# A two-part transformer block in fp32: a stage's first tile pair block by block, output projections opened with three column tiles by parts, the last products of the conv layer in token halves

## What is computed

```python
def first_block(x, ...):                        # two layers, h = h + rmsnorm(y)
    y = dilated_mixer(rmsnorm(h), w_in, w_out)  # proj = u @ w_in (10240 columns); rope; windowed attention
                                                # y = o * silu(gate);  y @ w_out
    y = diff_mixer(rmsnorm(h), w_in, ..., w_out)  # differential attention, 8 heads; norm of the heads; y @ w_out
def second_block(x, ...):                       # two layers, x = layer_norm(ALPHA * x + y) twice
    y = hybrid_mixer(x, ...)                    # sparse attention (top 128 keys) and a gated linear recurrence
                                                # merged @ w_out + b_out
    y = conv_ffn(x, ...)                        # u = conv3(x @ w_up) + conv_b; (gelu(a) * b) @ w_down, d_ff 2816
```

## Time and profile before

| | us |
|---|---|
| median of 3 runs (lowest, highest) | 2964.12 (2963.4, 2969.92) |
| the profiled execution, its own time | 2959.03 |
| its span | 2957.7 |
| PE busy | 2789.0 (94%) |
| DVE, ACT, POOL busy | 1241.4, 1106.9, 1069.7 |

### The profile page before, as it was taken

How to read it: one execution, slowest core, us unless ns; L and a number is a source line. 1 busy time by engine, 2 the same in 40 slices (tenths; PEclk the granted TensorE clock), 3 DMA queues, 4 the chain that set the end, 5 groups by cost and what they waited for, 6 DMA issues and landing times.

```text
span 2957.7 us, 39008 instructions
## 1 busy us (share of the span) xinstructions
PE 2789.0 (94%) x15161; PEld 2291.5 (77%) x15161; DVE 1241.4 (42%) x2777; ACT 1106.9 (37%) x2069; POOL 1069.7 (36%) x854
## 2 busy tenths in 40 slices
PE   6999999989989899999899999999999989999997
PEld 5887878788768777766688888887776668888887
DVE  3344444444454437423325424255642332642425
ACT  3444444443444433443322433233335232242422
POOL 3333333223322233332344354435342235434442
PEclk9999999999999899999999999999999999999999
DMA  4322223241211222222244232323222224322222
GB/s 142 90 83 86 87 72 100 73 138 44 72 58 44 79 92 85 72 79 82 92 154 137 72 114 72 100 86 120 72 72 79 89 82 157 125 84 100 93 93 72
DMA packets 247547, 269.06 MB, mean 91 GB/s; under 512 B 11582, under 2 KB 208930, under 8 KB 246596
## 3 DMA queue, kind: packets, MB, share of 16 engines
q1 hardware_dynamic: 247364, 266.56, 27.7%
HBM read 247.59 MB, written 18.94 MB: 90 GB/s over the span
## 4 chain that ended last, share of the span: by engine, by line
PE 80%; DVE 8%; ACT 4%; POOL 3%; issue 3%; DMA 2%; SPq 0%; ACTq 0%; DVEq 0%; POOLq 0%
PE banks L1458 43%; PE banks L1455 24%; POOL WS L2685 3%; DVE AR L2118 2%; PE banks L1577 2%; PE banks L1476 2%; PE banks L1526 1%; PE banks L1684 1%; ACT WS L1784 1%; PE banks L1560 1%; DVE SM L2118 1%; PE banks L1500 1%; PE banks L1732 1%; PE banks L1662 1%; PE banks L1545 1%
## 5 line engine op out<-in xcount | busy, mean ns | idle before, releaser
L2685 POOL TENSOR_TENSOR WS<-WR,WS 128x512 fp32r<-128x512 f32 (+1 forms) x772 | 975.1, 1295 | 1579.6 <-ACT WS L1784 1579.6
L1458 PE MATMUL banks<-WS,UT 128*128 128x512 f32 (+1 forms) x5712 | 1218.1, 363 | 22.5 <-issue 5.5
L1458 PEld LDWEIGHTS banks<-WS,UT 128*128 128x128 f32 x5712 | 921.6, 192 | 199.8 <-issue 61.1
L1455 PE MATMUL banks<-UT,WS 128*128 128x512 f32 (+1 forms) x2928 | 690.9, 394 | 0.6 <-issue 0.6
L1455 PEld LDWEIGHTS banks<-UT,WS 128*128 128x128 f32 (+1 forms) x2928 | 547.8, 189 | 128.1 <-issue 13.5
L1784 ACT ACTIVATE WS<-WR 128x1024 fp32r<-128x1024 f32 (+2 forms) x408 | 395.1, 1021 | 121.0 <-PE banks L1458 63.2
L1458 PE MATMUL banks<-WS,AT 128*128 128x256 f32 (+1 forms) x1776 | 307.2, 334 | 20.3 <-DVE AT L2118 20.3
L1458 PEld LDWEIGHTS banks<-WS,AT 128*128 128x128 f32 x1776 | 267.9, 193 | 56.5 <-DVE AT L2118 15.8
L2648 DVE SCALAR_TENSOR_TENSOR AR<-banks,AR 128x511 f32<-128x511 f32 x88 | 66.0, 750 | 226.5 <-ACT AR L2098 226.5
L2118 DVE TENSOR_TENSOR AR<-AR 128x256 f32<-128x256 f32 (+2 forms) x165 | 144.9, 898 | 21.3 <-DMA AR<-spill 12.6
L2700 POOL TENSOR_TENSOR SM<-SM 128x1 f32<-128x1 f32 (+2 forms) x44 | 45.9, 1044 | 275.9 <-DVE SM L2624 120.5
(11 more groups left out here) (207 smaller groups left out, 2657.6 us busy)
## 6 DMA issues: line engine op xcount, KB each, us to landing
WR<-in_w_in SPq DMA_DIRECT2D x56, 1024.0 KB, 5.1
WR<-in_w_up SPq DMA_DIRECT2D x44, 1024.0 KB, 5.1
WR<-in_dil_w_in SPq DMA_DIRECT2D x128, 256.0 KB, 3.9
WR<-in_w_down SPq DMA_DIRECT2D x16, 1024.0 KB, 4.9
WR<-in_dil_w_in SPq DMA_DIRECT2D x8, 1024.0 KB, 5.2
WR<-in_diff_w_in SPq DMA_DIRECT2D x16, 512.0 KB, 4.3
WR<-in_diff_w_in SPq DMA_DIRECT2D x8, 1024.0 KB, 5.5
spill<-AR SPq DMA_DIRECT2D x32, 256.0 KB, 2.4
```

Of the source, the lines that this page charges most:

```text
L1455: mm = pe.matmul(B[bank][0:c, :], w[x][:, kk, g * P:g * P + c], act[:, y, kk, :], start=start, stop=stop)
L1458: mm = pe.matmul(B[bank][:, off:off + n], act[:, x, before_k + kk, g * P:g * P + P], w[y][:, kk, :], start=start, stop=stop)
L2685: ge.tensor_tensor(slot(i, 1)[:, s], raw(i)[:, s], slot(i, 0)[:, s].bitcast(F32), ALU.subtract).then_inc(lo_p.sem, 1)
```

## The change

`wide` with `fresh` now does both tiles of the pair for one block before it goes to the next. The second tile is opened at the first block, without splitting ahead. The next block's transposes stand in the middle of the second tile's products. Ropes follow each block.

`gates` issues the chunk transposes 0 to 3 four and six ticks after the gate tiles that they need (`soon`), within the attention's steps; the other four go to `by_blocks`.

`by_blocks` opens three column tiles for block 0: row blocks 0 to 3 of each, with a chunk transpose ahead of the first and behind each of the three, then row blocks 4 and 5 of the three, then 6 and 7, then the fourth tile whole. The third and the fourth tile are opened, and so split, earlier.

In `ffn` the last b tile (`f0b10`, `f1b10`) goes by halves of 256 tokens (`last`, `conv_last`); the banks of `f0d2` and `f1d2` are taken in the order 2, 3, 0, 1.

```diff
-    def open(self, name):
+    def open(self, name, ahead=True):
...
-        self.fill(min(self.limit, i + LOOK + last))
+        self.fill(min(self.limit, i + LOOK + last) if ahead else i + 1)
+        if not ahead:
+            self.soon(4, lambda: self.fill(min(self.limit, i + LOOK)))
...
+        if fresh:
+            self.turned(first)
+            for b in range(first, NB):
+                for half in range(2):
+                    if half and b == first:
+                        self.open(name, ahead=False)
+                    self.bank[i + half, b] = ((start + b) % 4, 0)
+                    self.step("mm", i + half, b, 0, 2)
+                    if half and b < 3:
+                        self.turned(b + 1)
+                    self.tick()
+                    yield 1
+                    self.step("mm", i + half, b, 2, 4)
+                    if half and b % by == by - 1:
+                        deal(i + 1, b // by)
...
-    def by_blocks(self, names, finish, late):
+    def by_blocks(self, names, finish, between=(), order=(0, 1, 2, 3)):
...
-                for j in range(2):
+                for what in between[:1]:
+                    self.step(*what)
+                for j in range(3):
                     ws.append(self.open(names[j]))
                     self.bank[ws[j], b] = (banks[j], 0)
-                    early[j] = self.tiles[ws[j]][1] - 2
-                    self.step("mm", ws[j], b, 0, early[j])
-                late()
+                    self.step("mm", ws[j], b, 0, 4)
+                    for what in between[j + 1:j + 2]:
+                        self.step(*what)
+                for k in range(4, self.tiles[ws[0]][1], 2):
+                    for j in range(3):
+                        self.step("mm", ws[j], b, k, k + 2)
+                early = [None, None, None, 0]
...
+                    if half and j < 2:
+                        self.soon(4, lambda: self.step("chunk", name, 2 * j))
+                        self.soon(6, lambda: self.step("chunk", name, 2 * j + 1))
             yield from self.token_major(f"{name}{j}", deal)
-            if j == 2:
-                for c in range(4):
-                    self.step("chunk", name, c)
-                    yield 1
-        for c in range(4, 6):
-            self.step("chunk", name, c)
-            yield 1
...
+            if (kind, j) == ("b", 10):
+                i = self.open(f"f{l}b10")
+                for half in range(2):
+                    for c in range(2):
+                        self.bank[i, c, half] = 2 - 2 * half + c
+                        self.step("last", l, i, c, half)
+                        self.step("conv_last", l, i, c, half)
+                        self.tick(2)
...
+                elif kind == "conv_last":
+                    l, i, c, half = a
...
+                    se.activation(d, B[order.bank[i, c, half]][:, 0:256], ACT.Identity, scale=cp[:, 2, f:f + 1],
+                                  bias=cp[:, 3, f:f + 1]).then_inc(conv_id.sem, 1)
+                    se.wait_ge(prod.sem, prod.at[l, 10, c, half])
+                    se.activation(AT[:, 0, 4 + c, s], d, ACT.Copy).then_inc(prod_hi.sem, 1)
```

More of the change, by code:

```diff
@@ L525, in layer1 @@
         self.fill(self.opened + 2)
-        self.by_blocks([f"l1o{j}" for j in range(4)], self.residual("l1o"), lambda: self.last_quarter("l1g", late))
+        for x in late:
+            self.step("times", *x)
+        self.by_blocks([f"l1o{j}" for j in range(4)], self.residual("l1o"), [("chunk", "l1g", c) for c in range(4, 8)])
     def layer2(self):
@@ L579, in layer2 @@
         self.fill(self.opened + 2)
-        self.by_blocks([f"l2o{j}" for j in range(4)], self.residual("l2o"), lambda: self.last_quarter("l2g", late))
+        for x in late:
+            self.step("times", *x)
+        self.by_blocks([f"l2o{j}" for j in range(4)], self.residual("l2o"), [("chunk", "l2g", c) for c in range(4, 8)])
     def hybrid(self, l):
@@ L759, in hybrid @@
         self.soon(1, lambda: self.step("load_gains", l))
[L760 removed]
+        self.by_blocks([f"m{l}o{j}" for j in range(4)], finish)
     def ffn(self, l):
@@ L788, in finish @@
                 self.turn_later("n", b, 8)
-        self.by_blocks([f"f{l}d2{c}" for c in range(4)], finish, lambda: None)
+        self.by_blocks([f"f{l}d2{c}" for c in range(4)], finish, order=(2, 3, 0, 1))
 def build(nc, ap, out):
```

99 lines of the change are left out of this document (74 added, 25 removed).

## The result

| | before | changed |
|---|---|---|
| median of 20 runs (lowest, highest) | 2964.32 (2956.64, 2969.92) | 2970.3 (2960.41, 2977.54) |
| ratio, 95% interval | | 1.0019 (1.0011, 1.0027) |
| the profiled execution, its own time | 2959.03 | 2977.54 |
| its span | 2957.7 | 2976.2 |

The change costs 0.19%, 5.6 us by the ratio (the medians differ by 6.0). The two profiled executions differ by 18.5 us, three times as much: the one of before is 5.3 under its median, the one of the changed kernel is the slowest of 20. So the traces are not compared by their ends, but stage by stage, and over several executions.

What follows compares the result with a forecast made beforehand. PE was taken as the bound, busy 2789.0 of 2957.7 us. The terms summed to +0.1 us won, 2958.9 against the traced 2959.03, or 2964.0 at the median; range 2954 to 2974.

Steps and rivals of the forecast that it cites:

- the rivals "slower": Chunk transposes holding banks in the attention, 2975.8 us (0.17); DVE meeting POOL, 2971.0 us (0.06).
- Item 1: First pair, l1a0: second tile needed after 12 products, a new wait of 5.0 us; -6.0, between -7.5 and -4.
- Item 3: l2a0: transposes no longer wait 2.18 us for the norm, heads add 1.5 of bank waits; +1.8, between 0 and +3.
- item 7: f0 by halves: ACT's four rounds delay the fourth tile, PE waits 4.7 us; -3.7, between -5 and -1.5.
- The rival on POOL and DVE: About eight more DVE meetings with POOL on the path, 0.88 us each, 7.0 in all: 2971.0 us; chance 0.06.
- Item 6: m0o held by its fourth tile either way, -0.2; m1o has 24 products behind its third tile's start, -2.9.
- Items 2 and 4: l1o +2.6, l2o +2.9: chunk transposes move into the attention, with waits of 2.5 and 1.5 us set there.
- the 15.8 of the rival: Chunks in the attention hold banks it needs: 15.8 us of waits over both layers, 2975.8 us; chance 0.17.
- Item 5: m0iq: wait of 3.32 us goes, second tile ready at 1061.8, +3.1; m1iq has no such wait, +0.5.
- Item 8: f1 by halves: weights there well before, wait of 7.14 us falls to 5.0; +2.0, between 0 and +4.
- the pattern named under "Sum": Across the ten terms: waits for activations go, and the weights of one tile more are waited for instead; sum +0.1.

Runs made afterwards that it cites:

- the parts that won alone: Changed kernel with l1a0, l2a0 in old order, m0o, m1o, f0d2 opened by two tiles, f0b10 at full width; 2956.95 us, ratio 0.9984 to before.

## Why the prediction was wrong

It said 2964.0, no change at 0.52, slower at 0.23. The kernel is 0.19% slower, with an interval from 0.11% to 0.27%: its middle is just inside the bound of 0.2%, but a loss is clear. 2970.3 lies in the range of 2954 to 2974; the sum near zero was wrong by some 6 us, the way that the rivals "slower" had it. The stage table has -9.1 where the sum had +0.1, and l2a0 is the largest part of the 9.2 between them.

- **Item 1, l1a0: right.** -6.0 forecast, -5.4 found, by the wait named (5.83 us for 5.0), with the two waits of 1.1 for the banks (1.07 each), and not given back. Its first sentence has a slip that does not enter the sum: in the old order the second tile is needed after 48 products, not 36.
- **Item 3, l2a0: the step that failed.** +1.8 forecast, -2.0 found. The text had the transposes' 2.18 go and set 1.5 for the heads' bank waits. What it left out is that by the new order the head transposes wait for the *rope*, that the rope on DVE stands behind the very row of the norm whose wait was to go (1.58 us), and that it now meets the next tile's split on POOL (the other 1.96 of 3.54). Behind the longer wait the next transposes ran at the low clock, 1.11 and 1.91 us instead of 0.66 and 1.03. With the split moved away the stage took 59.9 and 59.7 us, 1.5 under the old order, which is near the +1.8. Rows 15 showed such a meeting (1.57 against 0.69), and I priced it in item 7 alone. The rival on POOL and DVE had the right mechanism, at 0.06, but no meeting in l2a0 among its eight; its place was here, and it costs 2.0 us for two operations, not 0.88 for one. The Trainium skill, "SBUF — State Buffer", section "Who interferes with whom", has the rule, that a DVE instruction with two SBUF inputs contends with a GpSimd instruction that reads SBUF, and the trace agrees: 2.74 us against 0.76.
- **Item 6, m1o: undersized.** -2.9 forecast, -3.9 found (-5.1 between the two traces first compared). The count of 24 products was right, but I took the third tile as ready when it was in the old trace. It stood one raw buffer behind POOL's first tile, and POOL took 7.04 us for that one instead of 6.05 (7.04 also where m1o was opened with two tiles, so this is not the third tile's doing); PE then waited 8.44 for EX. The experiment that took POOL out of this chain took the wait out.
- **Items 2 and 4, l1o and l2o: right way, too large.** +2.6 and +2.9 forecast, +1.9 and +1.6 found. The waits in the projections came near what was said. In l1o, counted from the end of l1a0, POOL began the third tile not 3.6 us earlier but 0.6, and took 5.00 instead of 6.72, so that two errors partly cancel. The moved chunks cost more in the attention than the 4.0 us of waits I set: 2.61 and 0.55 us in l1, 2.23, 1.66 and 1.46 in l2, 8.5 in all, of which 5.4 name the chunks' low part (`AT`). That is twice my 4.0, and still far from the 15.8 of the rival.
- **Item 5, m0iq and m1iq:** +3.1 and +0.5 forecast; +1.4 (the stretch from m0's input to o0) and +0.6 found. The wait of m0iq was right to 0.1 us. Of the 1.7 that I counted as won beside it, some 0.7 came by the first two traces: the transposes do run at the higher clock (1.04 us for 1.91), but the 30 products behind the wait took 8.64 where warm ones take 7.0 at 0.234 each.
- **Item 6, m0o:** -0.2 and -0.5.
- **Item 7, f0: right.** -3.7 forecast and found, by ACT's rounds, shown by itself.
- **Item 8, f1: half.** +2.0 and +0.9. I took the weights to be there well before; PE waits 4.44 for EX. And what I gave to the half-width chain is nothing: full width does as well, since EX comes later than either.

So the pattern named under "Sum" was the right one, weights waited for instead of activations. The errors lay on one side but for l1a0 and m1iq, where they are 0.6 and 0.1. In l2a0, m1o and f1 they have one cause: where I had not traced the split of the next tile to its end, I took it as ready, or as beside nothing. That the total lies in the range although the mechanism in l2a0 was not in the sum is due to the range's width, not to foresight.

## What to carry to other kernels

When an opening is spread over more weight tiles, follow the last of them back, through its split, its raw buffer and the engine that frees this buffer: the wait for activations that is saved is paid again there. An operation that gets onto the path must be priced with what runs beside it, not alone: beside POOL two DVE operations that read both inputs from SBUF took 2.74 us here, and 0.76 without it. And a change of ten local parts is worth splitting: all together gave +0.2%, the parts that won alone -0.2%. The best mixture, with l1a0 and l2a0 in the old order, three tiles in every projection, DVE on m1o's third tile, the last chunk ahead of the fourth tile's split and all products at full width, gave -0.5%.

## What the runs showed that I had not expected

The same wait does not always cost the same. In the changed order of l2a0, PE's wait for the rope was 3.52 us in one execution and 3.53 in another. With two tiles in m0o and m1o:

```profile
725.56 1.12 PE L1588 MATMUL banks<-CT,AR 128*128 128x128 f32 x4 [3.52 <-DVE AR L2191]
...
729.03 1.91 PE L1562 MATMUL banks<-CT,AR 128*128 128x128 f32 x8
```

With f0b10 at full width:

```profile
726.47 0.66 PE L1582 MATMUL banks<-CT,AR 128*128 128x128 f32 x4 [3.53 <-DVE AR L2185]
...
728.35 1.03 PE L1556 MATMUL banks<-CT,AR 128*128 128x128 f32 x8
```

Behind the one the transposes ran at half the speed (1.12 and 1.91 us), behind the other at full (0.66 and 1.03): over 5 us from the end of the wait the granted clock is 0.50 in the one and 1.00 in the other. l2a0 took 64.5 and 61.6 us. With the 11 us at 0.54 in m1, which cost some 4 us, and the middle of m1, which took from 322.0 to 328.9 us by its clock with the same instructions, such falls are the likely source of most of the spread of 13 to 17 us between executions of one kernel; that was not tested by itself. It means that one profile is good to a few us only, and that a stage should be read in several.
